# Feed-forward norms applied after the gate-up product: a kernel for two layers of a hybrid block

## The reference, cut to what matters

```python
def rms_norm(x, g):
    y = x * lax.rsqrt(jnp.mean(x * x, axis=-1, keepdims=True) + EPS)
    return y * g

def swiglu_ffn(h, w_gu, w_down):          # D_MODEL 1024, D_FF 2816
    g, u = jnp.split(h @ w_gu, 2, axis=-1)
    return (jax.nn.silu(g) * u) @ w_down

for l in range(2):
    x = x + 0.5 * swiglu_ffn(rms_norm(x, ffn1_norm[l]), ffn1_w_gu[l], ffn1_w_down[l])
    h = rms_norm(x, mix_norm[l])
    ...                                   # h @ w_in[l]; a gated linear recurrence, a sparse attention
    ...                                   # with T5 position bias and a forgetting attention; merged
    x = x + merged @ w_out[l]
    x = x + memory_cross_attention(rms_norm(x, xattn_norm[l]), rms_norm(mem, mem_norm[l]), ...)
    x = x + 0.5 * swiglu_ffn(rms_norm(x, ffn2_norm[l]), ffn2_w_gu[l], ffn2_w_down[l])
return rms_norm(x, final_norm)
```

## Time and profile before

| | |
|---|---|
| median of 3 runs | 1520.07 us (1519.02 to 1524.56) |
| profiled execution | 1522.54 us, its span 1520.7 us |
| busy, share of the span | TensorE 95%, VectorE 62%, ScalarE 52%, GpSimd 3% |
| mean granted clock of TensorE | 0.984 of full speed |
| DMA | 243.6 MB, mean 160 GB/s |

### The profile page before, as it was taken

How to read it: one execution, slowest core, us unless ns; L and a number is a source line. 1 busy time by engine, 2 the same in 40 slices (tenths; PEclk the granted TensorE clock), 3 DMA queues, 4 the chain that set the end, 5 groups by cost and what they waited for, 6 DMA issues and landing times.

```text
span 1520.7 us, 26191 instructions
## 1 busy us (share of the span) xinstructions
PE 1448.3 (95%) x9061; PEld 1290.7 (85%) x9061; DVE 940.7 (62%) x1501; ACT 785.6 (52%) x1396; POOL 52.6 (3%) x124
## 2 busy tenths in 40 slices
PE   6999999899999999999999999998999999999997
PEld 5888889788889897888878888888898898888886
DVE  5665655678665555666566666467875565565664
ACT  5555555644544455445465555456455445554553
POOL 1010000000000100000000000000000001000000
PEclk9999999899999999999999999999999999999999
DMA  7687655334424535566556666543353345356661
GB/s 224 192 201 218 201 150 157 117 116 141 138 91 162 192 112 163 173 189 193 167 175 186 193 185 199 158 141 112 112 166 111 111 170 164 112 172 192 190 193 70
DMA packets 286088, 243.60 MB, mean 160 GB/s; under 512 B 14281, under 2 KB 263545, under 8 KB 285985
## 3 DMA queue, kind: packets, MB, share of 16 engines
q1 hardware_dynamic: 283856, 236.77, 51.4%
q10 hardware_dynamic: 1600, 4.25, 0.8%
q0 software_dynamic: 528, 1.26, 0.6%
HBM read 241.18 MB, written 1.27 MB: 159 GB/s over the span
## 4 chain that ended last, share of the span: by engine, by line
issue 90%; PE 5%; POOLq 2%; POOL 1%; DMA 1%; DVE 0%; ACTq 0%; ACT 0%; DVEq 0%
PE work L1492 2%; PE work L1494 1%; PE acc L1454 1%; POOLq L685 1%; POOL diag L686 1%; POOLq L680 1%; DMA fb<-in_forget_bias 0%; POOLq L682 0%; DMA rows_dram<-brow_dram 0%; PE acc L1392 0%; DMA brow_dram<-brow 0%; POOL t L699 0%; POOL rstd L683 0%; DVE brow L1131 0%; ACTq L829 0%
## 5 line engine op out<-in xcount | busy, mean ns | idle before, releaser
L489 DVE TENSOR_TENSOR w_lo<-raw,w_hi 128x1024 fp32r<-128x1024 f32 x444 | 532.3, 1220 | 167.7 <-ACT w_hi L481 166.8
L1492 PE MATMUL work<-act,w_hi 128*128 128x512 f32 x1408 | 497.0, 397 | 2.6 <-DVE act L1031 2.6
L481 ACT ACTIVATE w_hi<-raw 128x1024 fp32r<-128x1024 f32 x444 | 453.4, 1053 | 39.0 <-PE acc L1454 26.4
L1494 PE MATMUL work<-act,w_lo 128*128 128x256 f32 x1408 | 395.0, 281 | 0.0
L1417 PE MATMUL work<-act,w_hi 128*128 128x256 f32 x1696 | 319.5, 287 | 9.0 <-DVE o_lo L1291 5.3
L1492 PEld LDWEIGHTS work<-act,w_hi 128*128 128x128 f32 x1408 | 264.2, 188 | 66.8 <-DVE act L1031 1.8
L1417 PEld LDWEIGHTS work<-act,w_hi 128*128 128x128 f32 x1696 | 270.3, 194 | 15.8 <-issue 9.6
L1494 PEld LDWEIGHTS work<-act,w_lo 128*128 128x128 f32 x1408 | 266.0, 189 | 1.5
L1417 PE MATMUL work<-act,w_lo 128*128 128x256 f32 x848 | 241.4, 285 | 0.0
L1417 PEld LDWEIGHTS work<-act,w_lo 128*128 128x128 f32 x848 | 164.3, 194 | 0.1
L741 ACT ACTIVATE gu_s<-work 128x256 f32<-128x256 f32 x176 | 58.0, 382 | 201.7 <-PE work L1494 201.7
(11 more groups left out here) (222 smaller groups left out, 1725.2 us busy)
## 6 DMA issues: line engine op xcount, KB each, us to landing
raw<-in_ffn_w_gu SPq DMA_DIRECT2D x176, 512.0 KB, 5.0
raw<-in_w_in SPq DMA_DIRECT2D x52, 1024.0 KB, 5.2
raw<-in_ffn_w_down SPq DMA_DIRECT2D x44, 1024.0 KB, 5.0
raw<-in_w_branch SPq DMA_DIRECT2D x12, 1024.0 KB, 5.0
raw<-in_w_mkv SPq DMA_DIRECT2D x8, 1024.0 KB, 5.0
raw<-in_w_out SPq DMA_DIRECT2D x8, 1024.0 KB, 5.0
raw<-in_w_mq SPq DMA_DIRECT2D x4, 1024.0 KB, 5.1
raw<-in_w_mo SPq DMA_DIRECT2D x4, 1024.0 KB, 4.8
```

The source lines that it names most:

```text
L481: eng.activation(halves(w_hi, slot, kind, part), halves(raw, slot, kind, part), ACT.Copy)\
L489: eng.tensor_tensor(halves(w_lo, slot, kind, part), halves(raw, slot, kind, part), halves(w_hi, slot, kind, part).bitcast(F32), ALU.subtra ...
L1492: pe.matmul(work[:, 2 * c + g, :], w_hi[:, slot, at_w:at_w + P], act[:, :, k, :], start=(k == 0), stop=False, skip_group_check=True)
L1494: mm = pe.matmul(work[:, 2 * c + g, 0:SEQ], w_lo[:, slot, at_w:at_w + P], act_hi[:, k, :], start=False, stop=(k == KT - 1), skip_group_che ...
```

## The change

**The norms before ffn1 and ffn2.** TensorE transposes x itself (`raw_transposes`), and the gain is applied as before. The products gate and up are then of x times gain, without 1/rms. After the first tile TensorE makes 1/rms as a row (256 positions, the same on all partitions) by multiplying a matrix of ones by the two diagonal matrices (`rstd_rows`); ScalarE copies it out of PSUM. In each tile VectorE multiplies the gate by this row before SiLU (`scaled`). The up part is not multiplied; instead the residual is scaled by 0.5/rms of each position (`half_rstd`, made by GpSimd). Half of the transposed x goes to banks 2 and 3 of `work`. ScalarE squares the fourth quarter only after four of the eight gain multiplies (in the first feed-forward all squares come first, and the split of unit 0 after the gain multiplies).

**Layers.** The loops over the layers become Python loops, so the instructions of both layers are written out. The first unit of layer 1 is split at the end of ffn2 of layer 0.

**T5.** The 31 copies of the bias row are made by GpSimd after its first 1/rms.

```diff
@@ -452,7 +457,8 @@
         def ps2(name):
             if name[0] == "nt":
-                return acc2(name[2])
+                return acc2(name[2]) if name[1] in (1, 2) or name[2] < 2 else \
+                    work[:, name[2], :].rearrange("p (a b) -> p a b", a=2)
             return work[:, PLAN.bank[name], :].rearrange("p (a b) -> p a b", a=2)
         def acc2(s):
...
@@ -684,11 +691,17 @@
                 if diagonal:
                     g.drain()
                     e = g.tensor_scalar(diag[:, tt, :], ident[:], rstd[:, tt:tt + 1], None, ALU.mult)
+                    if n in (0, 5, 6):
+                        e = g.tensor_scalar(half_rstd[:, tt:tt + 1], rstd[:, tt:tt + 1], 0.5, None, ALU.mult)
                 e.then_inc(rstd_ready, 1)
             for tt in range(TT):
                 power(0, 0, tt)
-            g.wait_ge(brow_ready, 1)
+            g.wait_ge(consts_landed, 32)
+            for first, n, b in bucket_runs():
+                g.tensor_copy(brow[:, first:first + n], tab[:, b:b + 1].to_broadcast([HEADS, n]))
+            g.memset(brow[:, SEQ - 1 + P:SEQ + P], 0.0)
+            g.drain()
             g.wait_ge(job_done, PLAN.jobs[("ffn1", 2 * T5_PAIR, 1)] + 1)
             g.dma_start(brow_dram[:, :], brow[:]).then_inc(brow_stored, 16)
             g.wait_ge(brow_stored, 16)
...
@@ -778,7 +791,13 @@
                     for part in range(2):
                         nxt(at + 2, part, i)
-                tile(0)
+                gated(0)
+                a.wait_ge(row_done, 2 * l + (st == "ffn2") + 1)
+                a.activation(rstd_row[:], acc2(0)[:, 0, :], ACT.Copy).then_inc(row_ready, 1)
+                nxt(0, 0)
+                silu(0)
+                nxt(0, 1)
+                h_high(0)
                 triple(0)
                 with a.Fori(0, FFN_LOOP) as i:
                     triple(1, i)
...
@@ -831,10 +850,16 @@
             a.dma_start(tab[:], t["t5_bias"].rearrange("b h -> h b"), allow_slow_non_contiguous=True).then_inc(consts_landed, 16)
             a.dma_start(fb[:], t["forget_bias"].rearrange("l h -> h l"), allow_slow_non_contiguous=True).then_inc(consts_landed, 16)
-            with a.Fori(0, DEPTH) as l:
-                squares(l, 0)
-                first_split(l, 0)
-                norm_his(l, 0)
+            for l in range(DEPTH):
+                if l == 0:
+                    squares(l, 0)
+                    norm_his(l, 0)
+                    first_split(l, 0)
+                else:
+                    squares(l, 0, range(3))
+                    norm_his(l, 0, range(4))
+                    squares(l, 0, (3,))
+                    norm_his(l, 0, range(4, KT))
                 first_split(l, 1)
                 first_split(l, 2)
                 ffn(l, "ffn1")
...
@@ -1015,10 +1040,14 @@
                      .then_inc(o_part, 1)
                 splits(a, split_hi, l, "mv1")
                 splits(a, split_hi, l, "mo0")
-                squares(l, 3)
-                norm_his(l, 3)
+                squares(l, 3, range(3))
+                norm_his(l, 3, range(4))
+                squares(l, 3, (3,))
+                norm_his(l, 3, range(4, KT))
                 splits(a, split_hi, l, "mo1")
                 ffn(l, "ffn2")
+                if l + 1 < DEPTH:
+                    first_split(l + 1, 0)
             squares(DEPTH, 0)
...
@@ -1037,11 +1066,12 @@
                 for k in range(KT):
                     norm_lo(l, n, k, act_hi, act_lo, ("nt", n, k // 2), order)
-            def residual(l, st, scale):
+            def residual(l, st, scale=None):
                 for b in range(2 * TT):
                     cols = slice((b % 2) * 512, (b % 2) * 512 + 512)
                     v.wait_ge(acc_done, l * 16 + (4 * st + b + 1))
-                    v.scalar_tensor_tensor(out=x[:, b // 2, cols], in0=acc[:, b // 2, cols], scalar=scale,
+                    v.scalar_tensor_tensor(out=x[:, b // 2, cols], in0=acc[:, b // 2, cols],
+                                           scalar=half_rstd[:, b // 2:b // 2 + 1] if scale is None else scale,
                                            in1=x[:, b // 2, cols], op0=ALU.mult, op1=ALU.add).then_inc(x_ready, 1)
             def ffn(l, st):
...
@@ -1052,6 +1082,13 @@
                         v.tensor_tensor(gu_s[:, c, g, :], gu_s[:, c, g, :], work[:, 2 * c + g, 0:SEQ], ALU.add)\
                          .then_inc(bank_free[2 * c + g], 1)
+                def scaled(no, i=0):
+                    c = no % 2
+                    v.drain()
+                    if no == 0:
+                        v.wait_ge(row_ready, 2 * l + (st == "ffn2") + 1)
+                    v.tensor_tensor(gu_s[:, c, 0, :], gu_s[:, c, 0, :], rstd_row[:], ALU.mult).then_inc(gate_ready, 1)
+
                 def product(no, i=0):
                     c = no % 2
                     v.drain()
...
@@ -1126,26 +1166,22 @@
-            v.wait_ge(consts_landed, 32)
-            for first, n, b in bucket_runs():
-                v.tensor_copy(brow[:, first:first + n], tab[:, b:b + 1].to_broadcast([HEADS, n]))
-            v.memset(brow[:, SEQ - 1 + P:SEQ + P], 0.0)
-            v.drain().then_inc(brow_ready, 1)
             v.wait_ge(setup_pe, 1)
             v.tensor_copy(gains[:].rearrange("p n l k -> p (n l k)"), work[:, 0, 0:80])
             v.drain().then_inc(vec_ready, 1)
-            with v.Fori(0, DEPTH) as l:
+            for l in range(DEPTH):
                 v.tensor_copy(gain[:], gains[:, :, bass.ds(l, 1), :].rearrange("p n o k -> p n (o k)"))
                 v.drain().then_inc(gain_ready, 1)
-                for part in range(2):
-                    split_lo(v, l, (0, 0, 0), part)
                 norm_los(l, 0, 0)
+                if l == 0:
+                    for part in range(2):
+                        split_lo(v, l, (0, 0, 0), part)
                 for c in (1, 2):
                     for part in range(2):
                         split_lo(v, l, (c, 0, c), part)
                 ffn(l, "ffn1")
-                residual(l, 0, 0.5)
+                residual(l, 0)
                 norm_los(l, 1, 1)
                 splits(v, split_lo, l, ("ffn1", RING * PAIRS - 1))
...
@@ -1371,7 +1407,10 @@
                 norm_los(l, 3, 4)
                 splits(v, split_lo, l, "mo1")
                 ffn(l, "ffn2")
-                residual(l, 3, 0.5)
+                if l + 1 < DEPTH:
+                    for part in range(2):
+                        split_lo(v, l + 1, (0, 0, 0), part)
+                residual(l, 3)
             v.wait_ge(final_gain_landed, 16)
             for tt in range(TT):
...
@@ -1403,6 +1442,26 @@
                         mm = rows_over_rms(l, ("nt", n, k // 2), k, tt, x)
                         if tt == TT - 1 and k % 2:
                             mm.then_inc(job_done, 1)
+
+            def raw_transposes(l, st, n):
+
+                for g in range(2):
+                    wait_tile_bank(pe, l, st, 1, g, 1)
+                for tt in range(TT):
+                    for k in range(KT):
+                        if k % 4 == 0 or (tt == 0 and k == 2):
+                            pe.wait_ge(x_ready, l * 16 + 4 * n + 2 * tt + (2 if k else 1))
+                        mm = pe.transpose(ps2(("nt", n, k // 2))[:, k % 2, tt * P:tt * P + P],
+                                          x[:, tt, k * P:(k + 1) * P], ident[:])
+                        if tt == TT - 1 and k % 2:
+                            mm.then_inc(job_done, 1)
+
+            def rstd_rows(l, st):
+
+                pe.wait_ge(rstd_ready, l * 12 + (12 if st == "ffn2" else 2))
+                for tt in range(TT):
+                    mm = pe.matmul(acc2(0)[:, 0, tt * P:tt * P + P], ones[:], diag[:, tt, :], start=True, stop=True)
+                mm.then_inc(row_done, 1)
             def columns(l, u, name, col, width, out_ps, x_hi, x_lo, kn, wait_k=None, last=True):
...
@@ -1503,8 +1562,11 @@
                         pe.wait_ge(h_lo_ready, l * (2 * FT) + i * 2 + (tile_no(st, 2 * no) + kk + 1))
                     sum_unit(l, ffn_unit(st, at, i), hi, lo, 0, at == 3, at == RING * PAIRS - 1, operand)
-                for at in range(3):
-                    gate_up(at)
+                gate_up(0)
+                rstd_rows(l, st)
+                gate_up(1)
+                gate_up(2)
+                pe.wait_ge(row_ready, 2 * l + (st == "ffn2") + 1)
                 down(3)
                 with pe.Fori(0, FFN_LOOP) as i:
                     gate_up(4, i)
```

More of the change, by code:

```diff
@@ L261, in block_kernel @@
         act_hi, act_lo = act[:, 0, :, :], act[:, 1, :, :]
-        junk = at("junk", [P, 2 * TT, 512], over="act")
         mem_x = at("mem_x", [P, TT, D])
@@ L288, in block_kernel @@
         mem_q = at("mem_q", [P, BT, SEQ], over="kc")
+        junk = at("junk", [P, 2 * TT, 512], over="qc")
         qi = at("qi", [P, BT, SEQ])
@@ L320, in block_kernel @@
         diag = at("diag", [P, TT, P])
+        ones = at("ones", [P, P])
         w_uk = at("w_uk", [P, BT, LAT])
```

(30 more changed lines are left out.)

## The result

The changed kernel takes 1508.95 us (median of 4 runs, 1508.47 to 1510.02) against 1519.82 us before (median of 4, the three shown and one more). The ratio is 0.9923, with a 95% interval of 0.9902 to 0.9944: 11 us less. The forecast was 1511.0, between 1506 and 1518. Timed again on another chip the ratio was 0.9917 (0.9893 to 0.9941).

A forecast was written before the change was run, and what follows sets the result against it. TensorE's own instructions bound the loops, leaving its waits at feed-forward starts. Terms 3.69 + 5.05 + 3.54 - 2.2 + 0.9 - 0.2 = 10.8 us, less 1.7 for clock, off 1522.54 gave 1513.4; median 2.5 lower: 1511.0, range 1506 to 1518.

The forecast's parts named there:

- Starts of ffn2: Before ffn2 in both layers: earlier, cheaper transposes of x start gate-up sooner, saving 3.69 and 5.05 us.
- Start of ffn1 in layer 1: Before layer 1's ffn1: no loop jump on VectorE and early transposes start gate-up at 765.64, saving 3.54 us.
- Rows of 1/rms: After each first gate-up tile: two fp32 matmuls on TensorE's path, some 0.55 us four times, costing 2.2 us.
- Start of the kernel: First gate-up at 17.0 instead of 20.18, less 2.25 us for a low clock: net +0.9 us.
- The multiply of the gate: VectorE's multiply in each of 88 tiles fits idle time before its next split: cost 0, cover 2.65 us.
- Rival 3: The gate multiply outgrows its cover and every tile pays: 52 us at worst, 1563 us; chance 0.04.
- Tail: At the final norm: GpSimd's extra half of 1/rms before the signal costs 0.2 us.
- The allowance for the clock: Three later feed-forward starts: 1.7 us taken off for one new low-clock spell of 3.4 us at half pace.
- Rival 1: The clock falls at each feed-forward start because transposes act as idleness: 1515.5 us; chance 0.25.
- rival 2: No low spell at later starts and the first gate-up at full clock: 1507 us; chance 0.17.
- From the profiled execution to the median: Whole-kernel time: 1513.4 from the profiled execution, with the median of the runs 2.5 us lower, gives 1511.0.

The follow-up runs named there:

- Experiment 4: Changed kernel with each transpose of x made by an ordinary float32 matmul against the identity; 1513.88 us, ratio 0.9952.
- experiments 1 and 2: Kernel before with layer loops written out: 1519.97 us, ratio 0.9989; then also with layer 1's first-unit split moved ahead of the residual: ratio 0.9953.
- second profile: Profile of the unaltered changed kernel when timed again on another chip beside the kernel before; ratio 0.9917.
- experiment 5: Changed kernel with three or six more unused VectorE multiplies per tile; 1511.11 us (ratio 0.993) and 1520.39 us (ratio 0.9984).
- experiment 6: Changed kernel with ten unused matmuls or twenty transposes after layer 0's first transposes of x; 1503.72 and 1504.44 us, one execution each.
- layers_and_t5: Kernel before with layer loops written out and the 31 T5 copies on GpSimd; 1515.68 us, ratio 0.9963.
- start_and_tail: Changed kernel with unit 0's split halves before and between the first gain multiplies, and no final-norm diagonal or half of 1/rms; 1502.91 us, ratio 0.9864.

## Why the prediction was right, point by point

- **Starts of ffn2.** Predicted 3.69 and 5.05 us (1.36 of the second from today's low spell), with gate-up 3.48 us after the last matmul. Measured 3.48 in both, 3.69 and 5.05 less. Experiment 4 splits the 3.69 into 1.14 for the instruction and 2.55 for the chain.
- **Start of ffn1 in layer 1.** Predicted 3.54, measured 3.64. The reason held: no jump, and the two causes, gains and transposes, ready together. The move of VectorE's split, which I named and costed at nothing, hides a cost: where the split stayed behind the residual it slowed GpSimd's diagonal to 2.21 us (experiments 1 and 2). In the changed kernel the diagonal is off the path, so the number was not touched.
- **Rows of 1/rms.** Predicted 2.2 us. The row matmuls start where the next tile would have, that tile starts 0.36 us later, and its first matmul takes 0.08 longer: 0.44 each where I had 0.55, 1.8 in all. The feed-forwards of layer 1 and 0 show it within their scatter (184.06 against 183.62).
- **Start of the kernel.** Predicted 17.0 for gate-up and 2.25 us for the clock, net +0.9. Measured 17.69 and 1.2 in the first profile, net +1.3; in the second 17.61 and 2.6, net nothing. Of the mechanism, the idleness of TensorE and the fall of the clock were right. The size of the fall's cost changes from one execution to the next, so that the first profile meets the term so closely is in part luck. What I didn't see is that the T5 copies alone, with the old norm, would bring 4 us, more than the whole of the changed start: the earlier start of TensorE (9.15 in place of 13.71) stands in the sum only for the transposes.
- **The multiply of the gate.** Predicted 0 with 2.65 - 0.6 = 2.0 us of cover; measured 1.80. Where VectorE stood idle 0.47 us before, the multiply now stands (741.03), and the next split follows at 741.40. Rival 3 is out by experiment 5.
- **Tail.** Predicted -0.2. GpSimd's last diagonal and VectorE's last multiply, which before the change began 0.66 us after it (1515.68 and 1516.34):

```profile
1501.49 0.62 POOL L693 TENSOR_SCALAR diag<-ident,rstd 128x128 f32<-128x128 f32 x1 [0.17 <-issue]
...
1502.33 1.28 DVE L1418 SCALAR_TENSOR_TENSOR final_out<-x,rstd,final_gain 128x1024 f32<-128x1024 f32 x1 [2.15 <-POOL half_rstd L695]
```

Now it is 0.84. With GpSimd's first operation for the second half at 0.90 us (0.74 before), beside VectorE's multiply of the other half, the tail grew by 0.3 (9.02 to 9.36).
- **The allowance for the clock.** I took off 1.7 us for a new low spell at one of three later starts. None occurred in any of the seven profiles with transposes of x: in 21 later starts the granted clock was 1.00 for the 6 us before and the 10 us after gate-up's first matmul. This was the term that failed: the transposes left only 1.3 us of idleness, and experiment 6 shows that they hold the clock. Rival 1 is out with it; rival 2, 1507, was half right.
- **From the profiled execution to the median.** The sum less the allowance gave 9.1 us off 1522.54, and I carried the whole 2.5 us between that execution and the median over to the new kernel. The profiled execution after the change lies 0.5 below its median. The terms measured add to 3.69 + 5.05 + 3.64 - 1.8 + 1.3 - 0.3 = 11.6 us; without the 1.36 us of a spell that only that execution is known to have, 10.2, and with the start of the second profile 8.9, against 10.9 between the medians. The profiles differ by 14.1; the other 2.5 us lie in the mixing parts and in ffn2, inside their scatter. So 1511.0 was 2 us high. The allowance is 1.7 of it; the errors of the rows and the tail are 0.4 and 0.1.

## What to carry to other kernels

Where a chain of small operations stands between two long stretches of matmuls, look for the factor that commutes with the product: per position 1/rms could be applied after gate-up and in the residual, and 2.5 us a start went, because the chain could run beside a whole tile. Price what an edit frees on each engine by itself, the small ones too; here moving 31 tiny copies off VectorE was worth 4 us with the old norm at the start, and the new norm there gave them back. And count how long TensorE idles after an early start of work: an order that keeps it fed was worth 3.6 us and a full clock (start_and_tail).

## What the runs showed of the hardware that I had not expected

- Transposes alone brought the clock up from the low pace (0.21 us each) to the full one (0.11), and a stretch of 20 more held it.
- A GpSimd operation of 128x128 took 2.21 us instead of 0.63 beside VectorE's subtraction of two SBUF tensors, and ended 0.4 us after it. The 31 copies took 4.1 us in the changed kernel, where VectorE had one input in PSUM meanwhile, and 6.1 in layers_and_t5 and 7.2 in start_and_tail, where splits of the same kind ran beside them.
- The jump back of a loop over the layers cost VectorE 2.38 us once, and its going was worth nothing at that start (7.11 to 8.40) until the next thing in the way was moved too, and then 0.3 us (6.81).
